# Neighbourhood attention: every second unit's probabilities turned by VectorE squares and a way through DRAM, its values product two steps later

## The chip, the cores and the metric

One Trainium2 chip, one of its cores. The kernel is a single program on that core, with every engine programmed by hand. The metric is the device time of one execution in microseconds (us), as the median of several runs. Engines are called PE (TensorE), DVE (VectorE), ACT (ScalarE), POOL (GpSimd) and SP (SyncE); SP and ACT can also issue DMAs.

## The reference, cut to what matters

The model is a block of four mixers (pool, neighbourhood attention, convolution, pool) followed by two transformer layers, all in float32 on 256 tokens of width 1024. The change is in the neighbourhood attention, which for 16 heads of width 64 computes:

```python
s_loc = s_loc + bias[None]                       # 256 local keys, with a relative position bias
s_ctx = jnp.einsum('brqhd,bchd->bhrqc', q, kc)   # 256 context keys
logits = jnp.concatenate([s_loc, s_ctx], axis=-1)
p = jax.nn.softmax(logits, axis=-1)
p_blk = jnp.einsum('bhrqij,qjk->bhrqik', p_loc, sel)
o = jnp.einsum('bhrqik,brikhd->brqhd', p_blk, vb) + jnp.einsum('bhrqc,bchd->brqhd', p_ctx, vc)
y = (o * jax.nn.silu(g)) @ w_out
```

Each head's probabilities (256 queries by 512 keys) multiply the values. A matrix product contracts over partitions, so the probabilities, computed with queries on partitions, must first be turned so that keys lie on partitions.

## The kernel before, in words

**The stretch.** `na_layer` exists three times, once for each of ACT (L888), PE (L1659) and DVE (L2370); the engines run their own programs in order and meet through semaphores. After the input projections, the attention runs as a software pipeline of 18 steps, `for i in range(NA_UNITS + 2)`. A unit is two heads (one pair `hp = u // 2`) by one half of the queries (`u % 2`), so there are 16 units, and a unit's logits are 128 partitions by 1024 columns: two heads `c`, each with 256 local and 256 context keys.

**Step i on PE.** `na_scores(i)` (L1615) computes the logits of unit i into banks 4 and 5; `gate_part(i)` (L1717) does a part of the gate's projection; `na_turned(i - 2)` (L1630) turns unit i-2's probabilities by eight 128x128 transposes (L1636) into banks 6 and 7; `na_values(i - 3)` (L1640) multiplies unit i-3's turned probabilities, now in `pt`, with the values (eight matmuls, L1655). In step 8 the gate part comes last. After steps 16 and 17 and a few gate transposes, `out_group` begins the output projection.

**Step i on DVE.** It adds the bias to the local logits of unit i and writes them to a row buffer (L2452), takes the negative maximum (L2456), copies half of unit i-2's turned probabilities from bank 6 to `pt` (`turned`, L2399), takes a reciprocal (L2403), and copies unit i-3's values product out (`values`, L2392). Steps 10 and 12 have a piece of the gate's scaling ahead of `turned` (`gate_scaled`, L2426).

**Step i on ACT.** It copies unit i's context logits to the row buffer (L904), takes the exponentials of unit i-1 (two of 512 columns, L912), copies the other half of unit i-2's turned probabilities from bank 7 to `pt` (L923), and in even steps takes one weight group apart (`split`, L654). Steps 7 and 15 have a part of the gate (L885).

**Buffers.** Row buffers are three, taken by `u % 3`; `pt` holds two units, taken by `u % 2`, so that the copies of unit u wait for the values product of unit u-2:

```python
act.wait_ge(pe_done, pe_s.count(("na_t", u, 1)))
if u >= 2:
    act.wait_ge(pe_done, pe_s.count(("na_out", u - 2)))
act.activation(pt[:, (u % 2) * 1024 + 512:(u % 2) * 1024 + 1024], ps[:, 7, :],
```

**The bias.** SP's queue loads the bias of a head pair in eight DMAs of 64 KB with rows of 256 bytes (`load_bias`, L446) into one of two halves of `bias`. The half for pair j+2 is loaded once the addition of unit 2j+1 is done (L565), POOL then adds the mask to it (L623), and DVE's addition of unit 2j+4 waits for that. Between them SP sends the output weights (`raw<-in_na_w_out`, 512 KB each) and, at two places (j = 1 and 3), a table of 1280 + 256 KB from DRAM to DRAM (`keep_rel`, L530). The last of the kernel's weights follow as slots come free.

## Time and profile before

| | us |
|---|---|
| median of 3 runs | 1818.37 (1818.0 to 1819.73) |
| span of the profiled execution | 1816.7 |
| busy: PE | 1797.5 (99%) |
| busy: POOL, DVE, ACT | 1365.0, 942.8, 905.1 |
| the 18 steps of the attention | 303.1 to 374.7 of the span |

The span runs from the first to the last instruction of the one execution that was taken with a profile; that execution's time as the runs are timed is not recorded, so the span and the median stand beside each other: 1816.7 and 1818.37. The chain of waits is the profile's answer to what ended last: it is followed back from the last instruction, at each step to what released it. TensorE's granted clock is 1.00 of full speed (2.4 GHz) in each ten-microsecond stretch from 300 to 390 us. In the views a "wait" names what ended the idle time just before an instruction.

### The profile page before, as it was taken

The numbers are of one execution on the slowest core, as the hardware profiler recorded it, in microseconds if no ns is written. First come the engines' busy times: TensorE is split into PE (matmuls) and PEld (weight loads), VectorE is DVE, ScalarE is ACT, GpSimd is POOL, SyncE is SP. The second block draws the span as 40 slices with busy tenths as digits, with TensorE's granted clock in tenths as the row PEclk, the third lists the DMA queues.
The fourth block names the chain that finished last, engine by engine and source line by source line (L and its number), as shares of the span: only waits on it lengthen the run. The fifth ranks groups of instructions, "written<-read, shape, count | busy, mean of one in ns | idle before, by whom it ended". The sixth has DMA issues, their size and how long they took to land.

```text
span 1816.7 us, 25068 instructions
## 1 busy us (share of the span) xinstructions
PE 1797.5 (99%) x9322; PEld 1482.3 (82%) x9322; DVE 942.8 (52%) x1756; ACT 905.1 (50%) x1337; POOL 1365.0 (75%) x568
## 2 busy tenths in 40 slices
PE   6999999999999999999999999999999999999999
PEld 5888888887889888887888888888888878888887
DVE  4673766678655524776553230714095865143152
ACT  3334424764456644455554644464445565545442
POOL 2624544559868898987689798969897858888885
PEclk9999999999999999999999999999999999999999
DMA  9853885748775775565466566567655645656653
GB/s 366 299 201 93 278 301 164 196 157 301 245 279 188 221 216 194 172 209 165 132 187 195 175 195 195 193 184 232 195 195 181 186 139 163 194 160 211 190 194 128
DMA packets 200697, 366.61 MB, mean 202 GB/s; under 512 B 32868, under 2 KB 54356, under 8 KB 200020
## 3 DMA queue, kind: packets, MB, share of 16 engines
q1 hardware_dynamic: 197568, 357.39, 61.6%
q10 hardware_dynamic: 3028, 7.86, 1.1%
q8 instruction: 65, 1.06, 0.2%
q14 instruction: 36, 0.29, 0.0%
HBM read 364.12 MB, written 6.13 MB: 204 GB/s over the span
## 4 chain that ended last, share of the span: by engine, by line
PE 98%; DMA 0%; ACTq 0%; ACT 0%; DVE 0%; POOL 0%; issue 0%; DVEq 0%
PE ps L1258 26%; PE ps L1260 26%; PE ps L1259 26%; PE ps L1384 3%; PE ps L1385 3%; PE ps L1386 3%; PE ps L1949 1%; PE ps L1951 1%; PE ps L1950 1%; PE ps L1306 1%; PE ps L1876 1%; PE ps L1655 1%; PE ps L1626 1%; PE ps L1636 1%; PE ps L1516 1%; PE ps L1921 1%
## 5 line engine op out<-in xcount | busy, mean ns | idle before, releaser
L616 POOL TENSOR_TENSOR w_lo<-raw,w_hi 128x1024 fp32r<-128x1024 f32 x556 | 1346.0, 2458 | 403.4 <-ACT w_hi L654 382.2
L1258 PE MATMUL ps<-w_hi,act_rows_r 128*128 128x512 f32 x2064 | 814.8, 395 | 3.2 <-POOL w_lo L616 3.1
L1260 PE MATMUL ps<-w_hi,act_rows_r 128*128 128x512 f32 x2064 | 804.8, 390 | 0.0
L1259 PE MATMUL ps<-w_lo,act_rows_r 128*128 128x512 f32 x2064 | 804.5, 390 | 0.0
L654 ACT ACTIVATE w_hi<-raw 128x1024 fp32r<-128x1024 f32 x556 | 571.1, 1058 | 359.4 <-DMA raw<-in_ffn_w_up 96.5
L1258 PEld LDWEIGHTS ps<-w_hi,act_rows_r 128*128 128x128 f32 x2064 | 387.9, 188 | 89.9 <-issue 8.6
L1260 PEld LDWEIGHTS ps<-w_hi,act_rows_r 128*128 128x128 f32 x2064 | 387.8, 188 | 81.8
L1259 PEld LDWEIGHTS ps<-w_lo,act_rows_r 128*128 128x128 f32 x2064 | 388.1, 188 | 77.2
L2604 DVE STREAM_TRANSPOSE ps<-proj 32x256 f32<-32x256 f32 (+1 forms) x384 | 166.6, 434 | 6.5
L2585 DVE TENSOR_TENSOR proj<-proj,ps 128x1024 f32<-128x1024 f32 (+1 forms) x18 | 20.4, 1132 | 252.2 <-PE ps L1260 247.8
L1384 PE MATMUL ps<-act_rows_r,w_hi 128*128 128x512 f32 (+1 forms) x288 | 101.4, 352 | 0.0
L1385 PE MATMUL ps<-act_rows_r,w_lo 128*128 128x512 f32 (+1 forms) x288 | 100.3, 348 | 0.0
L1386 PE MATMUL ps<-act_rows_r,w_hi 128*128 128x512 f32 (+1 forms) x288 | 100.2, 348 | 0.0
L1384 PEld LDWEIGHTS ps<-act_rows_r,w_hi 128*128 128x128 f32 x288 | 54.4, 189 | 8.3 <-issue 1.4
L1386 PEld LDWEIGHTS ps<-act_rows_r,w_hi 128*128 128x128 f32 x288 | 54.4, 189 | 7.0
L1385 PEld LDWEIGHTS ps<-act_rows_r,w_lo 128*128 128x128 f32 x288 | 54.4, 189 | 6.6
L2924 DVE TENSOR_TENSOR proj<-proj,ps 128x1024 f32<-128x1024 f32 x12 | 14.7, 1221 | 85.3 <-PE ps L1951 85.3
L2223 DVE SCALAR_TENSOR_TENSOR x_res<-ps,x_res 128x512 f32<-128x512 f32 x23 | 15.8, 689 | 77.3 <-PE ps L1260 77.3
L1056 ACT ACTIVATE proj<-ps 128x1024 f32<-128x1024 f32 x20 | 20.6, 1028 | 64.7 <-PE ps L1260 64.7
L985 ACT ACTIVATE proj<-ps 128x1024 f32 (+1 forms) x15 | 15.4, 1028 | 71.2 <-PE ps L1260 71.2
L2587 DVE SCALAR_TENSOR_TENSOR proj<-ps,rstat,proj 128x512 f32<-128x512 f32 (+1 forms) x12 | 7.9, 703 | 76.2 <-PE ps L1260 74.6
L2070 DVE SCALAR_TENSOR_TENSOR ps<-pt,cond,ps 128x512 f32<-128x512 f32 x60 | 45.3, 755 | 3.5 <-DMA pt<-in_ada_w 0.2
(245 smaller groups left out, 1559.9 us busy)
## 6 DMA issues: line engine op xcount, KB each, us to landing
raw<-in_w_in SPq DMA_DIRECT2D x120, 512.0 KB, 3.8
raw<-in_ffn_w_gate SPq DMA_DIRECT2D x88, 512.0 KB, 4.3
raw<-in_ffn_w_up SPq DMA_DIRECT2D x88, 512.0 KB, 4.3
raw<-in_ffn_w_down SPq DMA_DIRECT2D x88, 512.0 KB, 3.4
proj<-in_ada_w SPq DMA_DIRECT2D x39, 512.0 KB, 7.8
pt<-in_ada_w SPq DMA_DIRECT2D x38, 512.0 KB, 6.4
raw<-in_pool_w_in SPq DMA_DIRECT2D x32, 512.0 KB, 7.4
raw<-in_na_w_in SPq DMA_DIRECT2D x32, 512.0 KB, 5.4
```

The source lines that it names most:

```text
L616: pool.tensor_tensor(w_lo[:, s, :], raw[:, s, :], w_hi[:, s, :].bitcast(F32), ALU.subtract).then_inc(lo_done, 1)
L654: act.activation(w_hi[:, g % SLOTS, :], raw[:, g % SLOTS, :], ACT.Copy).then_inc(hi_done, 1)
L1056: act.activation(pj(MIX_ORDER[n] * 512, 512, IN_COLS), pair_of(n), how).then_inc(acc_free[(b + n) % 2], 1)
L1258: pe.matmul(o, h, hi, start=start, stop=False)
L1259: pe.matmul(o, h, lo, start=False, stop=False)
L1260: return pe.matmul(o, c, hi, start=False, stop=stop)
L1384: pe.matmul(o, weights_of(w_hi), high, start=start, stop=False, skip_group_check=True)
L1385: pe.matmul(o, weights_of(w_lo), high, start=False, stop=False, skip_group_check=True)
L1386: return pe.matmul(o, weights_of(w_hi), low, start=False, stop=stop, skip_group_check=True)
L2070: last = dve.scalar_tensor_tensor(out=to, in0=w, scalar=scale, in1=acc, op0=ALU.mult, op1=ALU.add)
L2585: return dve.tensor_tensor(h, h, ps[:, at:at + 2, cols_of], ALU.mult)
L2604: last = dve.transpose(to, rows)
```

## The change

`NA_SQUARED = (0, 2, 4, 6, 8, 10)` names six of the 16 units. For such a unit u:

- PE's eight transposes in step u+2 are left out, and with them both copies to `pt`.
- In their place DVE, in step u+2, turns the unit's 128x1024 probabilities by squares of 32x32 within each quadrant of partitions, one instruction, from the row buffer to `bias[:, 2048:3072]`.
- ACT, in step u+3, issues one DMA of 512 KB from there to a DRAM buffer `na_squares` (`keep_squares`), once the squares are made and the last unit's squares have come back.
- ACT, in step u+4, waits for that DMA and issues four DMAs of 128 KB with runs of 1 KB, each to 32 partitions of a buffer in `proj` (`place_squares`), which puts the squares where a full turn would.
- PE's values product of u comes in step u+5, not u+3, and waits for the four. Step 15 holds two products, of units 10 and 12; for unit 10 the output goes to bank 3.
- ACT's copy of context logits in step u+3 reuses the row buffer and waits for the squares.
- SP waits for all six DMAs to DRAM before the load of the gate rows into the same part of `bias`.

```diff
-            return 2 if u < NA_UNITS - 3 else 4
+            return 3 if u == NA_SQUARED[-1] else 2 if u < NA_UNITS - 3 else 4
+        def na_due(i):
+            return [u for u in range(NA_UNITS - 1) if u + (5 if u in NA_SQUARED else 3) == i]
...
+            sp.wait_ge(na_kept, 16 * len(NA_SQUARED))
             gate_rows(1, ((bias, 2048),), 4 * max(ADA_AT["na_in"].values()) + 3)
...
+                def keep_squares(u):
+                    act.wait_ge(dve_done, dve_s.count(("na_sq", u)))
+                    if u:
+                        act.wait_ge(na_placed, 64 * (u // 2))
+                    act.dma_start(na_squares[:], bias[:, 2048:3072]).then_inc(na_kept, 16)
+                def place_squares(u):
+                    act.wait_ge(na_kept, 16 * (u // 2 + 1))
+                    if u:
+                        act.wait_ge(pe_done, pe_s.count(("na_out", u - 2)))
+                    for kq in range(4):
+                        act.dma_start(na_placed_rows([[256, 4], [1, 256]], 0, slice(32 * kq, 32 * kq + 32)),
+                                      bass.AP(na_squares.tensor, 256 * kq, [[1024, 32], [32 * 1024, 4], [1, 256]])).then_inc(na_placed, 16)
...
-                        if i >= 3:
+                        if i - 3 in NA_SQUARED:
+                            act.wait_ge(dve_done, dve_s.count(("na_sq", i - 3)))
+                        elif i >= 3:
                             act.wait_ge(pe_done, pe_s.count(("na_t", i - 3, 1)))
...
+                    if i - 3 in NA_SQUARED:
+                        keep_squares(i - 3)
+                    if i - 4 in NA_SQUARED:
+                        place_squares(i - 4)
...
-                        act.wait_ge(pe_done, pe_s.count(("na_t", u, 1)))
-                        if u >= 2:
-                            act.wait_ge(pe_done, pe_s.count(("na_out", u - 2)))
+                        if u not in NA_SQUARED:
+                            act.wait_ge(pe_done, pe_s.count(("na_t", u, 1)))
+                            if u >= 2:
+                                act.wait_ge(pe_done, pe_s.count(("na_out", u - 2)))
...
-                pe.wait_ge(dve_done, dve_s.count(("na_pt", u, 0)))
-                pe.wait_ge(act_done, act_s.count(("na_pt", u, 1)))
+                if u in NA_SQUARED:
+                    pe.wait_ge(na_placed, 64 * (u // 2 + 1))
+                else:
+                    pe.wait_ge(dve_done, dve_s.count(("na_pt", u, 0)))
+                    pe.wait_ge(act_done, act_s.count(("na_pt", u, 1)))
...
-                    if i >= 2:
+                    due = na_due(i)
+                    for u in due[:-1]:
+                        na_values(u)
+                    if i >= 2 and i - 2 not in NA_SQUARED:
                         na_turned(i - 2)
-                    if i >= 3:
-                        na_values(i - 3)
+                    for u in due[-1:]:
+                        na_values(u)
...
+                    if u in NA_SQUARED:
+                        dve.wait_ge(act_done, act_s.count(("na_e", u, 1)))
+                        if u:
+                            dve.wait_ge(na_kept, 16 * (u // 2))
+                        dve.transpose(free(bias[:, 0:1], [[32, 8], [256, 4], [1, 32]], 2048),
+                                      na_rows_of(u, [[P, 8], [32, 4], [1, 32]])).then_inc(dve_done, dve_s.one(("na_sq", u)))
```

The order of instructions moves at two places of note. The first is DVE in step 12, before (its addition, L2452, its maximum, the gate's scaling, the copy of unit 10, reciprocal, copy of a values product):

```order
L2452 TENSOR_TENSOR full<-ps,bias 128x2x256 [waits pe_done,act_done,bias_masked]
L2456 TENSOR_REDUCE stat<-full 128x2 [waits dve_done]
L2426 SCALAR_TENSOR_TENSOR proj<-proj,rstat 128x256 [waits dve_done,acc_free0]
L2426 SCALAR_TENSOR_TENSOR proj<-proj,rstat 128x256
L2399 COPY pt<-ps 128x512 [waits pe_done]
L2403 RECIPROCAL rstat<-stat 128x2 [waits act_done]
L2392 COPY proj<-ps 128x128 [waits pe_done]
```

and with the change:

```order
L2507 TENSOR_TENSOR full<-ps,bias 128x2x256 [waits pe_done,act_done,bias_masked]
L2511 TENSOR_REDUCE stat<-full 128x2 [waits dve_done]
L2481 SCALAR_TENSOR_TENSOR proj<-proj,rstat 128x256 [waits dve_done,acc_free0]
L2481 SCALAR_TENSOR_TENSOR proj<-proj,rstat 128x256
L2448 STREAM_TRANSPOSE bias<-full 128x8x4x32 [waits na_kept,act_done]
L2458 RECIPROCAL rstat<-stat 128x2 [waits act_done]
L2439 COPY proj<-ps 128x128 [waits pe_done]
```

The copy to `pt`, which waited for PE, has become the transpose by squares, which waits for unit 10's exponentials and for the earlier DMA to DRAM.

The second is ACT from the start of step 14 to the exponentials of step 15, before (L904 copies context logits, L912 are exponentials, L923 copies unit 12 to `pt`, L654 splits weights):

```order
L904 ACTIVATE proj<-ps 128x2x256 [waits pe_done]
L912 ACTIVATE full,stat<-full,stat 128x512 [waits dve_done]
L912 ACTIVATE full,stat<-full,stat 128x512
L923 ACTIVATE pt<-ps 128x512 [waits pe_done]
L654 ACTIVATE w_hi<-raw 128x1024 [waits raw_in4]
L904 ACTIVATE full<-ps 128x2x256 [waits pe_done]
L912 ACTIVATE proj,stat<-proj,stat 128x512 [waits dve_done]
L912 ACTIVATE proj,stat<-proj,stat 128x512
```

and with the change (the same are now L939, L947, L963 and L671):

```order
L939 ACTIVATE proj<-ps 128x2x256 [waits pe_done]
L947 ACTIVATE full,stat<-full,stat 128x512 [waits dve_done]
L947 ACTIVATE full,stat<-full,stat 128x512
L929 DMA proj<-na_squares 32x4x256 [waits pe_done,na_kept]
L929 DMA proj<-na_squares 32x4x256 x3
L963 ACTIVATE pt<-ps 128x512 [waits pe_done]
L671 ACTIVATE w_hi<-raw 128x1024 [waits raw_in4]
L939 ACTIVATE full<-ps 128x2x256 [waits pe_done]
L947 ACTIVATE proj,stat<-proj,stat 128x512 [waits dve_done]
L947 ACTIVATE proj,stat<-proj,stat 128x512
```

Ahead of unit 12's copy stand now the four DMAs that bring unit 10's squares back (two rows). The copy of unit 12 still waits for PE's values product of unit 10, which has moved from step 13 to step 15.

## Rows read from the trace of the kernel before

**Rows 1.** The page, part 4: the chain that ended last, by engine.

```profile
PE 98%; DMA 0%; ACTq 0%; ACT 0%; DVE 0%; POOL 0%; issue 0%; DVEq 0%
```

**Rows 2.** PE in order of time, one step: start us, us, engine, line, what.

```profile
321.24 0.39 PE L1626 MATMUL ps<-act_rows_r 64*128 64x256 f32 x2
323.64 1.04 PE L1636 MATMUL ps<-ident,full 128*128 128x128 f32 x8
324.60 1.09 PE L1655 MATMUL ps<-pt,proj 128*64 128x128 f32 x16
325.63 0.39 PE L1626 MATMUL ps<-act_rows_r 64*128 64x256 f32 x2
```

**Rows 3.** DVE in order of time, the additions that begin steps 5, 8, 9, 12, 13.

```profile
322.98 0.69 DVE L2452 TENSOR_TENSOR proj<-ps,bias 128x512 f32<-128x512 f32 x1 [1.33 <-ACT proj L904]
323.71 1.22 DVE L2456 TENSOR_REDUCE stat<-proj 128x2 f32<-128x1024 f32 x1
337.04 0.69 DVE L2452 TENSOR_TENSOR proj<-ps,bias 128x512 f32<-128x512 f32 x1 [1.08 <-POOL bias L623]
340.70 0.69 DVE L2452 TENSOR_TENSOR full<-ps,bias 128x512 f32<-128x512 f32 x1 [0.85 <-ACT full L904]
354.70 0.69 DVE L2452 TENSOR_TENSOR full<-ps,bias 128x512 f32<-128x512 f32 x1 [2.12 <-POOL bias L623]
356.57 1.06 DVE L2426 SCALAR_TENSOR_TENSOR proj<-proj,rstat 128x256 f32<-128x256 f32 x2
358.41 0.68 DVE L2452 TENSOR_TENSOR full<-ps,bias 128x512 f32<-128x512 f32 x1
```

**Rows 4.** Busy time by stretch: us, PE, PEld, DVE, ACT, POOL, clock, DMA share, GB/s.

```profile
323.70:331.60 7.90, 7.90 (x82) 6.53 (x81) 5.05 (x9) 5.25 (x12) 3.78 (x2) 1.00 0.71 230
341.40:349.00 7.60, 7.60 (x80) 6.29 (x79) 5.62 (x11) 4.95 (x11) 2.91 (x2) 1.00 0.98 216
```

**Rows 5.** POOL in order of time: the mask that step 12 waits for.

```profile
352.28 2.40 POOL L623 TENSOR_TENSOR bias<-bias,na_mask 128x1024 f32<-128x1024 f32 x1 [7.96 <-DMA bias<-na_rows]
```

**Rows 6.** VectorE transposes by form: busy us, mean ns | idle before.

```profile
L2604 DVE STREAM_TRANSPOSE ps<-proj 32x256 f32<-32x256 f32 x320 | 145.9, 456 | 5.6
L2604 DVE STREAM_TRANSPOSE ps<-proj 32x128 f32<-32x128 f32 x64 | 20.7, 323 | 0.9
```

**Rows 7.** DMA issues: out<-in, queue, count, KB each, median us to landing.

```profile
raw<-in_na_w_out SPq DMA_DIRECT2D x8, 512.0 KB, 3.8
bias<-na_rows SPq DMA_DIRECT2D x48, 64.0 KB, 2.7
out<-x_res SPq DMA_DIRECT2D x3, 256.0 KB, 2.0
proj<-in_decay ACTq DMA_DIRECT2D x4, 192.0 KB, 4.2
```

**Rows 8.** ACT and its DMA queue (ACTq) in order of time.

```profile
52.66 3.90 ACT L654 ACTIVATE w_hi<-raw 128x1024 fp32r<-128x1024 f32 x4 [1.55 <-issue]
834.85 0.45 ACTq L659 DMA_DIRECT2D proj<-in_decay  x1
834.92 0.40 ACT L1065 ACTIVATE full<-full,stat 128x128 f32<-128x128 f32 x1
```

**Rows 9.** ACT in order of time, steps 14 to 16.

```profile
364.44 0.60 ACT L923 ACTIVATE pt<-ps 128x512 f32<-128x512 f32 x1 [0.45 <-PE ps L1636]
364.94 1.05 ACT L654 ACTIVATE w_hi<-raw 128x1024 fp32r<-128x1024 f32 x1
366.37 0.60 ACT L904 ACTIVATE full<-ps 128x512 f32<-128x512 f32 x1 [0.39 <-PE ps L1626]
370.98 0.20 ACT L912 ACTIVATION_READ_ACCUMULATOR full<-full,stat 128x1 f32 x1
```

**Rows 10.** PE in order of time: the start of step 15, and what follows the loop.

```profile
365.36 0.38 PE L1626 MATMUL ps<-act_rows_r 64*128 64x256 f32 x2
374.74 0.50 PE L1258 MATMUL ps<-w_hi,act_rows_r 128*128 128x512 f32 x1
```

More of the change, by code:

```diff
@@ L86 @@
 NA_UNITS = 16
+NA_SQUARED = (0, 2, 4, 6, 8, 10)
 NA_Z_BANK = (3, 5, 6, 7)
@@ L169, in program @@
     rel_rows = nc.dram_tensor("rel_rows", (LAYERS, P, REL_PITCH), F32, kind="Internal").ap()
+    na_squares = nc.dram_tensor("na_squares", (P, 1024), F32, kind="Internal").ap()
     gate_scratch = nc.dram_tensor("gate_scratch", (DEPTH, KC, 2, P), F32, kind="Internal").ap()
@@ L230, in program @@
         decay_in = sem("decay_in")
+        na_kept, na_placed = sem("na_kept"), sem("na_placed")
         out_done = sem("out_done")
@@ L298, in na_out_bank, with na_last_of, na_placed_rows @@
         def na_out_bank(u):
-            return 2 if u < NA_UNITS - 3 else 4
+            return 3 if u == NA_SQUARED[-1] else 2 if u < NA_UNITS - 3 else 4
+        def na_due(i):
+            return [u for u in range(NA_UNITS - 1) if u + (5 if u in NA_SQUARED else 3) == i]
+        def na_last_of(k):
+            return 4 * k + 2 if 4 * k + 2 in NA_SQUARED else 4 * k + 3
+        def na_placed_rows(dims, at=0, rows=slice(0, P)):
+            return free(proj[rows, 0:1], dims, CTX_RES + D + at)
         def na_rows_of(u, dims, at=0):
@@ L919, in na_layer @@
                         u = i - 2
-                        act.wait_ge(pe_done, pe_s.count(("na_t", u, 1)))
-                        if u >= 2:
-                            act.wait_ge(pe_done, pe_s.count(("na_out", u - 2)))
-                        act.activation(pt[:, (u % 2) * 1024 + 512:(u % 2) * 1024 + 1024], ps[:, 7, :],
-                                       ACT.Copy).then_inc(act_done, act_s.one(("na_pt", u, 1)))
+                        if u not in NA_SQUARED:
+                            act.wait_ge(pe_done, pe_s.count(("na_t", u, 1)))
+                            if u >= 2:
+                                act.wait_ge(pe_done, pe_s.count(("na_out", u - 2)))
+                            act.activation(pt[:, (u % 2) * 1024 + 512:(u % 2) * 1024 + 1024], ps[:, 7, :],
+                                           ACT.Copy).then_inc(act_done, act_s.one(("na_pt", u, 1)))
                         if i == NA_UNITS:
@@ L1654, in na_values @@
                         o = (u % 2) * 1024 + c * 512 + k * P
-                        last = pe.matmul(ps[c * HD:(c + 1) * HD, bank, 0:P], v, pt[:, o:o + P], start=k == 0, stop=k == 3)
+                        maps = na_placed_rows([[256, 4], [1, 32]], 32 * (4 * c + k)) if u in NA_SQUARED else pt[:, o:o + P]
+                        last = pe.matmul(ps[c * HD:(c + 1) * HD, bank, 0:P], v, maps, start=k == 0, stop=k == 3)
                 last.then_inc(pe_done, pe_s.one(("na_out", u)))
@@ L2395, in turned @@
                 def turned(u):
-                    dve.wait_ge(pe_done, pe_s.count(("na_t", u, 0)))
-                    if u >= 2:
-                        dve.wait_ge(pe_done, pe_s.count(("na_out", u - 2)))
-                    dve.tensor_copy(pt[:, (u % 2) * 1024:(u % 2) * 1024 + 512], ps[:, 6, :]).then_inc(dve_done, dve_s.one(("na_pt", u, 0)))
+                    if u in NA_SQUARED:
[4 more added lines that the diff above has]
+                                      na_rows_of(u, [[P, 8], [32, 4], [1, 32]])).then_inc(dve_done, dve_s.one(("na_sq", u)))
+                    else:
+                        dve.wait_ge(pe_done, pe_s.count(("na_t", u, 0)))
+                        if u >= 2:
+                            dve.wait_ge(pe_done, pe_s.count(("na_out", u - 2)))
+                        dve.tensor_copy(pt[:, (u % 2) * 1024:(u % 2) * 1024 + 512], ps[:, 6, :]).then_inc(dve_done, dve_s.one(("na_pt", u, 0)))
                     dve.wait_ge(act_done, act_s.count(("na_e", u, 1)))
@@ L2433, in gated @@
                     dve.wait_ge(pe_done, pe_s.count(("tp", "nag", 0, k)))
-                    dve.wait_ge(dve_done, dve_s.count(("na_o", 4 * k + 3)))
+                    dve.wait_ge(dve_done, dve_s.count(("na_o", na_last_of(k))))
                     z = ps[:, NA_Z_BANK[k], :].rearrange("p (c n) -> p c n", c=2)
@@ L2447, in na_layer @@
                         dve.wait_ge(pe_done, pe_s.count(("na_s", i)))
-                        if i >= 3:
+                        if i >= 3 and i - 3 not in NA_SQUARED:
                             dve.wait_ge(pe_done, pe_s.count(("na_t", i - 3, 1)))
@@ L2465, in na_layer @@
                         gate_made(7)
-                    if i >= 3:
-                        values(i - 3)
+                    for u in na_due(i):
+                        values(u)
                     if i == NA_UNITS // 2 - 1:
```

## The prediction

> **What bounds the kernel now.** I read the chain that ended last first: TensorE (PE) makes up 98% of it [rows 1], so only what shortens or stalls PE counts. The change touches one stretch, the 18 steps of the neighbourhood attention. In PE's order of time a step takes 4.39 us (321.24 to 325.63): scores and a gate part 2.40, the eight transposes 0.96, the values 1.03 [rows 2]. PE has no gap there. But two waits of VectorE (DVE) show who stands close behind. The additions that begin steps 8 and 12 stood idle 1.08 and 2.12 us for the bias that GpSimd masks [rows 3], and GpSimd in turn had waited 7.96 us for the bias loads [rows 5]. PE did not feel it: the addition of step 12 ended at 355.39, the scores of step 13 began about 1.2 us later (365.36 less two steps of 4.39). So PE bounds the stretch with the bias loads 1.2 us behind, and these loads have company: in their two slow stretches the DMA engines are busy 0.71 and 0.98 of the time [rows 4].
>
> **What is removed.** Eight transposes for each of six units: 6 x 0.96 [rows 2] = 5.8 us of PE. With them go six copies on DVE and six on ScalarE (ACT). If PE stayed the bound up to the end this would be the result; 0.2% of this kernel, 3.6 us, is about what a measurement tells from no change.
>
> **What is added, engine by engine.** *DVE*: a transpose of 128x1024 by squares. The trace has none so wide; 256 columns take 456 ns and 128 take 323 [rows 6], so 1.04 ns a column and 0.456 + 768 x 0.00104 = 1.25 us. Below it is bounded by 1.0, above by 2.4 (if it had to sit out a GpSimd operation of 2.40 us [rows 5]); the slope is the nearest, I take 1.25. It replaces a copy of about 0.6, so a pair of steps gains 0.65 us on DVE, which idles 1.33 before a plain step's addition [rows 3]: covered in plain steps. *ACT*: five DMA issues per squared unit, 0.45 us each. In the row beside it ACT computes during an issue, but four in a row left it idle for 1.55 us where nothing was queued [rows 8]. Here two exponentials stand ahead of them, and a copy of 0.6 has gone: I cost the issues at 0 (bounds 0 and 1.55 a unit; the latter would show in the slack of ACT, not at once on PE). *DMA queues*: 512 KB out and 512 KB back per squared unit, beside what SyncE's queue carries (SyncE's own new wait stands after the last bias load, ahead of a 512 KB load that nothing near needs: 0).
>
> **The way through DRAM.** Out: between 2.0 us (256 KB to DRAM in a quiet stretch) and 4.2 (192 KB, four in a row on ACT's queue); the 512 KB loads in this stretch take 3.8, which I take, as it is the same size beside the same traffic. Back: the last of four issues comes 1.35 us after the first; a landing takes between 2.7 (64 KB) and 4.2 (192 KB), 128 KB lies halfway, 3.45 [rows 7]. Together 8.6 us. There are two steps and a piece: from the end of the squares to the values some 8.1 us (for unit 10, by the steps below: 357.4 to 365.5), and one trip per pair of steps of 8.78 - 0.96 = 7.8 us, since one DRAM buffer serves all. So the trip is itself nearly the bound. The stalls at steps 8 and 12 absorb the drift of the early trips; the last counts 8.6 + 0.1 - 8.1 = 0.6 us. Bounds: 0, and with 4.2 each way over five trips (9.75 - 7.8) x 5 = 9.7.
>
> The Trainium skill (DMA: Bandwidth & Descriptors, Anatomy of one DMA) gives 2.0 us plus bytes/436 GB/s for a DMA of GpSimd's path. Estimated by that page, out takes 3.2 and back 1.35 + 2.3, together 6.9 us, and the 0.6 above would be 0.
>
> **The chain through the bias.** Call l(i) the end of the addition of step i. The loads of the bias for steps 8 and 9 start when l(5) is done, those for 12 and 13 when l(9) is.
> - l(5): before, 323.67 [rows 3]. Step 2's transposes are gone by then, and step 4's: -1.9. But ACT's copy of step 5 now waits for the squares of unit 2: l(4), a step of 4.39 ahead of l(5), comes at 319.28 - 0.96 = 318.3, the maximum (1.22, of which 1.14 count, since it overlaps its neighbours) to 319.5, squares to 320.7, copy 321.35, addition: 322.1. So -1.6.
> - l(5) to l(8) is load, mask, addition: 14.06 us (337.73 - 323.67) and does not shrink with PE. l(8) = 336.2.
> - l(8) to l(9): maximum 1.14, squares 1.25, ACT's copy 0.65, addition 0.7: 339.9 (before 341.39).
> - l(9) to l(12): again load and mask, 14.0 (355.39 - 341.39): 353.9.
> - l(12) to l(13): maximum 1.14, the gate's scaling 1.06 [rows 3], squares 1.25, copy 0.6, addition 0.7: 358.7, before 359.09.
>
> So of the 3.8 us that PE saves in steps 6 to 12 the bias gives back all but a little, and PE waits in steps 9 and 13.
>
> **The end of the loop.** Scores of step 14 start at 358.75, those of step 15 at 363.15 (before 365.36 [rows 10]): -2.2. Then a new wait. The copies of unit 12 (ACT and DVE, step 14) wait for the values of unit 10, as ever two units back; but these are now computed in step 15 and not 13. Values of unit 10: 363.15 + 2.40 + 1.03 = 366.6. Behind that wait ACT holds the copy of unit 12 (0.5), a weight split (1.05 [rows 9]) and the copy of step 15, which starts at 368.15 (before 366.37). From that copy to the end of unit 15's exponentials ACT worked without a gap for 4.8 us (366.37 to 371.18 [rows 9]): 372.95. Transposes 0.96, values 1.03: what follows the loop starts at 375.0, before at 374.74 [rows 10]: **+0.3**.
>
> **What the two share.** The new traffic meets the bias loads. At 230 GB/s and share 0.71 [rows 4] 512 KB cost all 16 engines 524/324 = 1.6 us, so the two transfers that fall into one bias load up to 3.2 us, and 0 if the engines' free time takes them. At share 0.98 there is none free: 2.0 us; at 0.71 most is: 1.0 us. Both lie on the chain above, whole: +3.0 (bounds 0 and 6.4).
>
> The Trainium skill (DMA: Bandwidth & Descriptors, Issuing engines are not separate DMA queues) says that DMAs of different issuers run on the same 16 engines and interleave, which speaks against hiding this traffic on ACT's queue. By that rule the +3.0 stands; without it the sum would be +0.9. No row here shows the two queues side by side in this stretch.
>
> **Sum**: +0.3 + 3.0 + 0.6 = +3.9 us. The profiled execution's span of 1816.7 becomes 1820.6; the runs' median, 1818.4, lies 1.7 above that span, which I take as unchanged: **1822.3 us**.
>
> **The rivals.**
> 1. *Forecast*: bias chain, tail wait, some contention. +1.5 to +6.4. Chance 0.47.
> 2. *The DMA engines have room*: shares are means, and 256-byte packets may be waiting rather than working (216 GB/s at 0.98 against 230 at 0.71). Then +0.3 to +0.9: 1819.0. For it: light stretches between loads. Against: 0.98. Chance 0.24.
> 3. *Faster*: the bias chain shrinks with PE, because its loads then overlap the other traffic less; the place is the addition of step 12. PE is free up to step 15 and only the tail wait is paid: step 15's scores at 365.36 - 5.76 = 359.6, values of unit 10 at 363.0, and by the steps above what follows at 371.4 or so: -3.3, 1815.1; it decides if the bias lands 3 us sooner after l(9). Without the tail wait too, -5.8: 1812.6. Against: 14.06 and 14.0 us in both chains. Chance 0.08.
> 4. *The trip is longer than its time*: landings of 4.2 and more each trip; PE waits before the values products of squared units, +7 to +10: 1827. For it: one DRAM buffer, and the bias loads beside it. Chance 0.16.
> 5. *Squares sit out GpSimd*: 2.4 instead of 1.25 us, three on the chain (steps 4, 8, 12), +3.5 more: 1826. Chance 0.05.
>
> **How the numbers follow.** The time is the forecast's. Faster by over 0.2% (below 1814.8): about half of rival 3, 0.04. Within 0.2%: the rest of it, rival 2 and some 0.16 of the forecast, below +3.6: 0.44. Slower (above 1822.0): the rest, 0.52. The range leaves one tenth on each side: from 1816.0 (most of rival 3 below) to 1828.5 (all but the end of rival 4).
>
> **What would show it.** PE's idle time before the scores of steps 9 and 13, released by DVE's addition and that by GpSimd's mask, 1 to 3 us each. ACT's copy of unit 12 waiting for a values product of PE, 3 us. l(5) to l(8) and l(9) to l(12) above 14 us. Squares at 1.25 us. Landings: out 3.8, back 3.5. I am wrong if PE waits instead for landed DMAs before the values in steps 5, 7, 11 (rival 4), or if these two intervals fall under 13 us (rival 3).

## The result, and the profile after

| | before | after |
|---|---|---|
| median of the runs, us | 1818.51 (4 runs, 1818.0 to 1819.73) | 1842.42 (4 runs, 1840.79 to 1847.01) |
| ratio | 1 | 1.0133 [1.0121, 1.0145] |
| span of the profiled execution, us | 1816.7 | 1845.2 (its own time 1847.01) |
| PE busy, us | 1797.5 | 1800.3 |

The change costs 23.9 us, where 3.9 were forecast and the range ended at +10. Six groups of transposes are gone, yet PE is busy 2.8 us longer, and the chain that ended last, 98% PE before [rows 1], is now 94% PE and 3% DMA (page, part 4):

```profile
PE 94%; DMA 3%; DVE 1%; ACT 1%; ACTq 1%; issue 0%; POOL 0%; DVEq 0%
```

**Where PE stood.** The waits of the stretch from 300 to 410 us (engine, what waited and for what, us in total, times, longest):

```profile
PE ps L1699 <- DMA proj<-na_squares: 19.2, 5, 8.5
ACT pt L963 <- PE ps L1699: 5.6, 1, 5.6
```

PE waited 19.2 us in five places for the rows that come back from DRAM. In PE's order of time (L1699 is a values product, L1676 and L1556 are transposes):

```profile
324.68 1.09 PE L1699 MATMUL ps<-proj 128*64 128x128 f32 x16 [1.74 <-DMA proj<-na_squares]
341.19 1.97 PE L1699 MATMUL ps<-proj 128*64 128x128 f32 x16 [8.52 <-DMA proj<-na_squares]
357.50 1.97 PE L1699 MATMUL ps<-proj 128*64 128x128 f32 x16 [6.74 <-DMA proj<-na_squares]
377.02 1.09 PE L1699 MATMUL ps<-proj 128*64 128x128 f32 x16 [1.69 <-DMA proj<-na_squares]
385.51 1.09 PE L1699 MATMUL ps<-proj 128*64 128x128 f32 x16 [0.51 <-DMA proj<-na_squares]
387.56 1.06 PE L1676 MATMUL ps<-ident,full 128*128 128x128 f32 x8 [0.95 <-DVE rstat L2458]
391.82 1.24 PE L1556 MATMUL ps<-ident,proj 128*128 128x128 f32 x8 [2.17 <-DVE proj L2439]
```

The last two waits, 3.1 us, are the tail of the loop. A values product takes 1.09 us [rows 2]; after the idle stretches of 8.52 and 6.74 us it takes 1.97. The granted clock says why (busy time by stretch: us, PE, PEld, DVE, ACT, POOL, clock, DMA share, GB/s), 1.00 before the long wait and 0.76 and 0.75 behind it, a mean of both levels, 2.4 and 1.2 GHz:

```profile
320.00:330.00 10.00, 8.26 (x86) 6.55 (x82) 6.21 (x11) 5.55 (x12) 5.15 (x3) 1.00 1.00 278
330.00:340.00 10.00, 2.67 (x18) 1.98 (x15) 3.37 (x6) 2.95 (x6) 2.47 (x3) 0.90 0.93 222
340.00:350.00 10.00, 8.80 (x71) 7.10 (x72) 5.97 (x11) 5.87 (x12) 5.90 (x3) 0.76 0.83 244
350.00:360.00 10.00, 3.26 (x29) 2.69 (x29) 2.31 (x5) 1.31 (x4) 1.56 (x2) 0.75 0.91 218
```

So a lost microsecond counts more than once: PE's busy time should have fallen by 5.8 and rose by 2.8. The Trainium skill (TensorE: Matmul & The Clock Gate, What's actually happening) names 1.2 GHz as the level of an idle array; the rows agree.

**Why the rows came late.** The chain of waits through this stretch, in order of time (start us, us, what):

```profile
324.71 9.34 DMA na_squares<-bias
334.07 0.31 ACTq L929
...
335.90 5.25 DMA proj<-na_squares
...
346.40 11.05 DMA proj<-na_squares
```

Unit 2 took 9.3 us out, 1.8 of issues, 5.3 back; unit 4's last quarter took 11.05 back. SP's queue shows what was under way at these two times (start us, us of issuing):

```profile
322.62 1.22 SPq L546 DMA_DIRECT2D rel_rows<-in_rel  x2
323.88 9.12 SPq L462 DMA_DIRECT2D bias<-na_rows  x8
345.08 1.17 SPq L546 DMA_DIRECT2D rel_rows<-in_rel  x2
```

L546 are the two copies of `keep_rel`, from DRAM to DRAM, issued within 2.1 us of the start of these two legs; behind them come bias loads. The issues of the stretch with their median landings:

```profile
na_squares<-bias ACTq DMA_DIRECT2D x6, 512.0 KB, 4.3
proj<-na_squares ACTq DMA_DIRECT2D x24, 128.0 KB, 3.7
rel_rows<-in_rel SPq DMA_DIRECT2D x2, 1280.0 KB, 9.4
```

The medians, 4.3 and 3.7, are close to the 3.8 and 3.45 that were forecast. Two of the six trips make 15.3 of the 19.2 us of waits.

**One wait far behind.** The profiled execution is the longest of the four. It holds one more wait of PE, of 2.83 us near 617 us, because one addition of DVE took 7.34 us (DVE in order of time):

```profile
609.94 7.34 DVE L3026 TENSOR_TENSOR proj<-x_res,act_rows 128x512 f32<-128x512 f32 x1
```

The same instruction takes at most 2.68 us in the trace of before, and again 7.34 us in two of the twelve experiments below (7 and 9). It belongs to the layer after, so I measure the attention by a landmark ahead of it: from the start of the first scores to the start of the last values product (unit 15). Before and after (PE in order of time):

```profile
303.13 0.38 PE L1626 MATMUL ps<-act_rows_r 64*128 64x256 f32 x2
...
380.41 1.09 PE L1655 MATMUL ps<-pt,proj 128*64 128x128 f32 x16
```

```profile
303.09 0.38 PE L1666 MATMUL ps<-act_rows_r 64*128 64x256 f32 x2
...
404.09 1.09 PE L1699 MATMUL ps<-pt,proj 128*64 128x128 f32 x16
```

That is 77.3 us and 101.0 us, +23.7, as much as the change in the medians (+23.9). PE waited 23.0 of the 101.0 us and worked 78.0; the same work took 72.6 us at a granted clock of 1.00 (experiment 8). So some 5.4 us of the loss are clock.

### The profile page after: what moved, and what is told of

It is laid out like the page before. It is cut to its first block, busy times and chain, and to the rows that moved or that the text cites. A ratio compares the mean times of both kernels' runs of the same rounds, so it can differ in the third digit from the quotient of the medians.

```text
span 1845.2 us, 24983 instructions
## 1 busy us (share of the span) xinstructions
PE 1800.3 (98%) x9274; PEld 1482.7 (80%) x9274; DVE 947.5 (51%) x1756; ACT 902.7 (49%) x1331; POOL 1364.4 (74%) x568
## 3 DMA queue, kind: packets, MB, share of 16 engines
q8 instruction: 65, 1.06, 0.2%
## 4 chain that ended last, share of the span: by engine, by line
PE 94%; DMA 3%; DVE 1%; ACT 1%; ACTq 1%; issue 0%; POOL 0%; DVEq 0%
PE ps L1298 25%; PE ps L1300 25%; PE ps L1299 25%; PE ps L1424 3%; PE ps L1425 3%; PE ps L1426 3%; PE ps L1996 1%; PE ps L1998 1%; PE ps L1346 1%; PE ps L1997 1%; DMA proj<-na_squares 1%; DMA na_squares<-bias 1%; PE ps L1923 1%; PE ps L1556 1%; PE ps L1968 1%; PE ps L1699 1%
## 5 line engine op out<-in xcount | busy, mean ns | idle before, releaser
L671 ACT ACTIVATE w_hi<-raw 128x1024 fp32r<-128x1024 f32 x556 | 571.5, 1058 | 380.1 <-DMA raw<-in_ffn_w_up 101.2
L2270 DVE SCALAR_TENSOR_TENSOR x_res<-ps,x_res 128x512 f32<-128x512 f32 x23 | 15.9, 689 | 78.6 <-PE ps L1300 78.6
L640 POOL TENSOR_TENSOR bias<-bias,na_mask 128x1024 f32<-128x1024 f32 x8 | 19.1, 2388 | 46.8 <-DMA bias<-na_rows 46.8
```

Source lines behind the costliest of these rows:

```text
L671: act.activation(w_hi[:, g % SLOTS, :], raw[:, g % SLOTS, :], ACT.Copy).then_inc(hi_done, 1)
```

## The experiments

Every number of the first column is the landmark distance less the 77.3 of before; the second is the difference of the medians, measured on the same chip. PE's idle time is from 300 to 400 us. The landmark rests on one profiled execution each: the three kernels in which PE waits for nothing there (before, 3 and 6) agree within 0.03 us, but two kernels with the trip (5 and 9), whose programs are the same up to step 13, are 2.5 us apart by then. A difference of two or three microseconds between kernels with the trip is therefore no finding by itself.

| | landmark | median | ratio [95%] | PE idle | clock 300 to 400 |
|---|---|---|---|---|---|
| the change | +23.7 | +23.9 | 1.0133 [1.0121, 1.0145] | 23.1 | 0.91 |
| 1 no trip | +7.6 | +7.4 | 1.0035 [1.0021, 1.0049] | 7.9 | 0.95 |
| 2 copies later | +14.5 | +24.4 | 1.0137 [1.0120, 1.0154] | 14.3 | 0.95 |
| 3 before, copies later | 0.0 | +8.4 | 1.0046 [1.0029, 1.0063] | 0 | 1.00 |
| 4 before, with the traffic | +5.6 | +6.6 | 1.0036 [1.0021, 1.0050] | 3.8 | 0.98 |
| 5 copies at the end | +16.3 | +16.3 | 1.0088 [1.0066, 1.0109] | 15.9 | 0.95 |
| 6 before, copies at the end | 0.0 | -0.4 | 0.9990 [0.9980, 0.9999] | 0 | 1.00 |
| 7 as 5, no trip | -1.0 | +2.1 | 1.0012 [1.0001, 1.0022] | 3.8 | 1.00 |
| 8 as 7, tail freed | -4.0 | -3.7 | 0.9984 [0.9974, 0.9994] | 0.8 | 1.00 |
| 9 as 5, tail freed | +8.2 | +12.1 | 1.0064 [1.0049, 1.0079] | 9.7 | 0.97 |
| 10 three units, u + 6 | +8.2 | +7.9 | 1.0043 [1.0029, 1.0057] | 7.0 | 0.97 |
| 11 three units, u + 5 | +4.9 | +6.3 | 1.0039 [1.0026, 1.0053] | 6.2 | 1.00 |
| 12 three units, u + 6, bank 3 | -0.1 | -0.4 | 0.9997 [0.9988, 1.0006] | 2.1 | 1.00 |

In the profiled executions of 7 and 9 the addition above took 7.34 and 7.35 us, in all others 2.7 or less; in 2 and 3 the loss behind the landmark has a cause of its own, told there.

**1. The way through DRAM taken out.** The five DMAs of a unit and their waits go; PE waits for the squares instead, and the products of the six units read what lies in the buffer, so their part of the output is not computed.

```diff
-                    act.dma_start(na_squares[:], bias[:, 2048:3072]).then_inc(na_kept, 16)
...
-                    for kq in range(4):
-                        act.dma_start(na_placed_rows(...), ...).then_inc(na_placed, 16)
...
-                    pe.wait_ge(na_placed, 64 * (u // 2 + 1))
+                    pe.wait_ge(dve_done, dve_s.count(("na_sq", u)))
```

> The change without its ten-DMA way: neither the DMA to DRAM nor the four back are issued, nobody waits for them, and the values products of the six squared units read what lies in the placed buffer (so their part of the output is not computed). Theory A (the trip through DRAM is what costs): PE's 40 us of waiting for na_squares goes, what is left is the forecast without contention, +0.3 us, so 1818 to 1821. Theory B (the rest of the change costs: squares on DVE, the bias loads behind the addition, the late values of unit 10): it stays above 1830.

1825.93 us (1822.99 to 1827.29), between the two theories. (The 40 us of the expectation add the waits of PE and of its weight loads, which overlap; PE waited 19.2.) The trip is 16.1 of the 23.7 us. But even without it the change is slower than before. The tail's two waits, 3.1 us, are still there, and another reason stands in two rows, POOL's mask for step 8 and the addition that it releases:

```profile
336.33 2.34 POOL L640 TENSOR_TENSOR bias<-bias,na_mask 128x1024 f32<-128x1024 f32 x1 [7.85 <-DMA bias<-na_rows]
338.70 0.69 DVE L2497 TENSOR_TENSOR proj<-ps,bias 128x512 f32<-128x512 f32 x1 [4.70 <-POOL bias L640]
```

PE waited 3.83 us for this addition. From l(5) to l(8) it is 17.0 us where I had kept 14.06. The addition of step 5 is done 1.3 us sooner than before, at 322.36, but SP's queue is still issuing a weight load and the two copies of `keep_rel`, and the bias load goes out at 323.83, as it did before (323.70). Its mask starts 12.5 us after that, where before it was 10.9.

**2 and 3. The copies of `keep_rel` moved** behind the convolution's first weights, in the change and in the kernel before.

```diff
-                if j in (1, 3):
-                    keep_rel(j // 2)
...
             gate_rows(2, ((pt, 0),), 4 * max(ADA_AT["cv_in"].values()) + 1)
+            keep_rel(0)
+            keep_rel(1)
```

> The change, with the two DRAM-to-DRAM table copies (1280 + 256 KB each) moved from the attention to after the convolution's weights. Theory A1 (the trips of units 2 and 6 are long because these copies and the bias loads fill the DMA engines): landings of the DMA to DRAM fall from 9.3 us at most to about 4.5, PE's waits of 8.5 and 6.7 us to about 2 each, and the time to about 1826. Theory A2 (a trip is too long for its two steps whatever runs beside it: 4.3 + 1.35 + 3.7 = 9.4 us against 7.8): the waits spread evenly, 1.5 us a unit, and the time is 1828 to 1832. Theory A3 (the copies play no part, the bias loads do): nothing changes, 1840.

> The kernel before, with the same two copies moved. PE was the bound with the bias 1.2 us behind, so all theories say no change, 1818 to 1819; what it gives is how long the bias takes from the addition to the mask without the copies: I expect 7 to 8 us in place of 10.9 for the third and fifth load.

1842.98 and 1826.98 us, neither as expected. The attention itself gains 9.2 us (23.7 to 14.5) with the copies away, but the place is a bad one: the kernel before loses 8.4 us by it while its attention is the same to 0.1 us. Its loss is for the most part a wait of PE for an operation of ACT, 6.0 us long, that ends at 519 us, in the layer after (5.7 in experiment 2). So these two medians say nothing of the change; the landmark does, and 5 and 6 repeat the pair with another place.

What 3 was made for came as expected. With the copies away, POOL's mask for step 8 starts 8.0 us after the bias load goes out (323.81), where before it was 10.9 (334.63 less 323.70), and that for step 12 after 7.0 instead of 10.9:

```profile
331.80 2.39 POOL L623 TENSOR_TENSOR bias<-bias,na_mask 128x1024 f32<-128x1024 f32 x1 [3.69 <-DMA bias<-na_rows]
```

**4. The traffic alone, beside the kernel before.** DMAs of the same sizes at the same steps, from and to buffers that nobody on PE or DVE waits for. The way back reads an input, and the way out has six buffers in DRAM, so it waits for nothing.

```diff
+                    if i - 3 in (0, 2, 4, 6, 8, 10):
+                        act.dma_start(na_squares[i // 2 - 1], bias[:, 2048:3072]).then_inc(na_kept, 16)
+                    if i - 4 in (0, 2, 4, 6, 8, 10):
+                        if i > 4:
+                            act.wait_ge(na_placed, 64 * (i // 2 - 2))
...
```

> The kernel before (all 16 units turned by PE) with the change's DMA traffic beside it and nobody on PE or DVE waiting for it: six DMAs of 512 KB from SBUF to DRAM on ACT's queue in steps 3 to 13 and six times four of 128 KB from DRAM in steps 4 to 14 (from an input, into a buffer nobody reads; each four wait for the four before). Forecast's contention term: the bias comes 1 to 2 us later in two places with 1.2 us to spare, so +1 to +3 us. Theory A1: the landings in steps 5 and 9 are 8 to 10 us here as well. If they are 4 us here, it is not the company that made them long in the change.

1825.13 us, +6.6 where +1 to +3 was expected. This is the disputed term by itself. The bias came later, and PE, bound by nothing before, now waited 3.23 us for an addition (POOL, DVE and PE in order of time):

```profile
339.23 2.34 POOL L626 TENSOR_TENSOR bias<-bias,na_mask 128x1024 f32<-128x1024 f32 x1 [10.02 <-DMA bias<-na_rows]
341.60 0.69 DVE L2463 TENSOR_TENSOR proj<-ps,bias 128x512 f32<-128x512 f32 x1 [5.46 <-POOL bias L626]
342.44 0.39 PE L1637 MATMUL ps<-act_rows_r 64*128 64x256 f32 x2 [3.23 <-DVE proj L2463]
```

Landings in this run (DMA issues, KB each, median us):

```profile
raw<-in_na_w_out SPq DMA_DIRECT2D x8, 512.0 KB, 6.9
bias<-na_rows SPq DMA_DIRECT2D x48, 64.0 KB, 5.2
na_squares<-bias ACTq DMA_DIRECT2D x6, 512.0 KB, 7.5
```

Against 3.8 and 2.7 of before [rows 7] both of SP's kinds of load take 2.5 to 3.1 us longer. The chains l(5) to l(8) and l(9) to l(12) are 18.5 and 16.5 us, 4.4 and 2.5 longer than before. The queues do share their engines, as the Trainium skill has it (DMA: Bandwidth & Descriptors, Issuing engines are not separate DMA queues); here the ways out don't wait for the trip before, as they do in the change, so that this kernel may well show more pressure on the bias than the change has. The way out took 10.2 us in step 5 and 8.6 in step 9, beside the copies, 6.5 to 7.7 in steps 7, 11 and 13, and 3.3 in step 3: the long leg does not need the change's own waits.

**5 and 6. The copies at the end of the attention's loads**, ahead of the convolution's weights, in the change and in the kernel before.

```diff
             keep_gates(2)
+            keep_rel(0)
+            keep_rel(1)
             narrow(I["conv_w_in"]
```

> The change, with the two DRAM-to-DRAM table copies moved to the end of the attention's sends, where the DMA engines are 0.2 to 0.3 busy (in the earlier place, after the convolution's weights, they cost 6 us of their own there). The earlier run's attention stretch had PE waits on landed squares of 3.7 us at most in place of 8.5, so: time 1842 - 24 + about 13 = 1830 to 1833. If the copies' company is not what makes the trips long, 1840 or more.

> The kernel before with the same move: PE is bound there, 1818 to 1819 if the new place costs nothing; a loss here has to be taken off the other three runs of this set.

1835.19 and 1818.56 us. The place is free this time, so the pair stands: without the company of the copies the loss is 7.5 us less. No landing of the trip is above 6.2 us now, and yet PE waits for five trips of six, four of them early ones (PE in order of time):

```profile
324.11 1.09 PE L1699 MATMUL ps<-proj 128*64 128x128 f32 x16 [1.29 <-DMA proj<-na_squares]
335.61 1.09 PE L1699 MATMUL ps<-proj 128*64 128x128 f32 x16 [3.51 <-DMA proj<-na_squares]
346.45 1.09 PE L1699 MATMUL ps<-proj 128*64 128x128 f32 x16 [1.32 <-DMA proj<-na_squares]
357.85 1.98 PE L1699 MATMUL ps<-proj 128*64 128x128 f32 x16 [3.41 <-DMA proj<-na_squares]
```

Pairs of steps follow at 11.5, 10.8 and 11.4 us here, by these rows, where 7.8 was to be had. That is the true length of a trip with one buffer. The next way out is issued 0.03 us after the values product starts (335.64, 346.48, 357.88), since both wait for the same four DMAs; so the round is the way out, the issues and the landing of the last quarter: 3.0, 1.8 and 6.0 us for the round that ends at 346.45. The last of the four landed after 4.9, 6.0 and 6.2 us in these three rounds, while the median of all 24 is 3.9.

The clock fell behind both long waits. Behind the one at 357.85 the values product is slow at once; behind the one at 335.61 it is the next product, and the two pairs of steps, less their waits, took 9.5 us each, against 8.0 behind the two waits of 1.3 us (PE, then busy time by stretch):

```profile
337.77 1.97 PE L1699 MATMUL ps<-pt,proj 128*64 128x128 f32 x16
```

```profile
338.00:340.00 2.00, 2.00 (x17) 1.67 (x16) 1.66 (x3) 1.88 (x5) 0.00 (x0) 0.50 0.69 140
358.00:360.00 2.00, 2.00 (x18) 1.67 (x20) 0.13 (x1) 0.60 (x1) 0.00 (x0) 0.50 0.86 276
```

One wait in this trace has another cause. In step 12 DVE's two scalings of the gate took 3.84 us, where the change has 0.75 and the kernel before 1.06 [rows 3], and PE waited for the copy behind them (DVE, then PE). Experiment 2 has the same, 3.86 and 2.04 us.

```profile
363.96 3.84 DVE L2481 SCALAR_TENSOR_TENSOR proj<-proj,rstat 128x256 f32<-128x256 f32 x2
369.34 1.09 PE L1699 MATMUL ps<-proj 128*64 128x128 f32 x16 [2.02 <-DVE proj L2439]
```

Without it the copies' company would come out some 2 us larger than 7.5.

**7 and 8. No trip, the copies at the end, and then the tail freed.** In 8 the copies to `pt` of unit u no longer wait for the values of unit u-2 where that is squared, since it has not used `pt`.

```diff
-                            if u >= 2:
+                            if u >= 2 and u - 2 not in NA_SQUARED:
                                 act.wait_ge(pe_done, pe_s.count(("na_out", u - 2)))
```

> No DMA out and back (the values of squared units read what lies in the placed buffer, so their part is not computed), and the copies at the end. With the copies beside it this was 1825.9, with 17.0 and 18.3 us between the additions of steps 5 and 8, and 7 and 10. Theory: the bias loads, not DVE's squares, were what PE waited for; without the copies the bias takes 8 us and no step waits for it, and only the late values of unit 10 are left of the loss: -5.8 + 3 to 4, so 1815 to 1817. If the squares on DVE or ACT's order cost by themselves: 1820 or more.

> As the run before, and the copies to pt no longer wait for the values of a squared unit two back (which doesn't use pt): this frees unit 12's copies in step 14 from the values of unit 10 in step 15. Theory (the tail's wait was worth 3 to 4 us of PE time): 1812 to 1813.5, the full 5.8 us of the transposes. If that wait was hidden: the same as the run before.

Both leave out the trip, and with it the six units' part of the output. 1821.02 us (1817.96 to 1825.19) and 1815.20 us (1814.44 to 1820.03), 4.0 and 1.7 us above the ends of what was expected. By the landmark the tail's wait is 3.0 us (-1.0 against -4.0), and the rows of 7 show it as PE's idle time in step 16 and behind it, with ACT's copy of unit 12 before (ACT, then PE):

```profile
363.43 0.60 ACT L955 ACTIVATE pt<-ps 128x512 f32<-128x512 f32 x1 [5.07 <-PE ps L1691]
364.27 1.06 PE L1668 MATMUL ps<-ident,full 128*128 128x128 f32 x8 [0.95 <-DVE rstat L2448]
368.54 1.07 PE L1548 MATMUL ps<-ident,proj 128*128 128x128 f32 x8 [2.17 <-DVE proj L2431]
```

The medians differ by 5.8. The profiled execution of 7 has the long addition of DVE on top, and its fastest execution is only 3.5 us above the fastest of 8; whether the addition makes the rest of the 5.8 in the executions without a profile isn't shown. Experiment 8 is what the removed transposes are worth when nothing takes their place: 4.0 us, not 5.8. From the first scores to those of step 15 six transposes and the one product put off should be 6.8 us less; it is 5.2. A later step without transposes takes 3.52 us, 0.87 less than 4.39 and not 0.96 (0.45 over five steps), and 1.2 are lost in steps 2 and 3, where PE runs into DVE's addition:

```profile
316.07 0.39 PE L1658 MATMUL ps<-act_rows_r 64*128 64x256 f32 x2 [0.48 <-DVE full L2497]
```

**9. As 5, with the tail freed.** The edit of 8 in kernel 5, the trip kept.

> The changed kernel with the two keep_rel copies moved behind keep_gates(2), as in the run that gave 1835.2, and besides the copies to pt no longer wait for a squared unit's values (they were in no need of it: a squared unit doesn't use pt). Theory A (the trip is late in each pair of steps and sets PE's time up to its last one; the wait of unit 12's copies is paid after that, on top of it): the 5.8 us that the same edit took away without the trip come off here too: 1829 to 1830. Theory B (the tail's wait lies beside the late trips; it costs only what the trips leave): 1832 to 1835, and PE's waits for the landed rows grow by what the tail's wait loses.

1830.75 us (1830.03 to 1832.13), 4.4 below the median of 5, with the long addition in its profile. The landmark fell by 8.1 us, from +16.3 to +8.2. Not all of that is the edit's. It touches the copies of unit 12 alone, in step 14, and from the first scores to the values product of step 13 it is 66.4 us in 5 and 63.8 in 9. These 2.5 us are scatter, most of it PE's wait for DVE in step 13 of 5. Behind that product it is 27.2 and 21.6 us. These 5.5 us can be the edit's: the tail's two waits (3.1), two waits of 0.2 and 0.4 ahead of them, and 1.9 of clock, which fell to 0.50 at 386 to 388 us in 5 and stayed at 1.00 in 9. In 7 the same two waits cost no clock (1.00 from 368 to 380). The last trips' waits of 9:

```profile
356.89 1.09 PE L1699 MATMUL ps<-proj 128*64 128x128 f32 x16 [2.44 <-DMA proj<-na_squares]
366.97 1.09 PE L1699 MATMUL ps<-proj 128*64 128x128 f32 x16 [0.57 <-DMA proj<-na_squares]
```

Against 8, which differs from 9 by the trip alone, the trip costs 12.2 us where neither the copies nor the tail add to it: 9.0 of waits and 3.2 of clock.

**10 and 11. Three units instead of six**, 0, 4 and 8, with the values at u + 6 and at u + 5, both with the copies at the end and the tail freed.

```diff
-NA_SQUARED = (0, 2, 4, 6, 8, 10)
+NA_SQUARED = (0, 4, 8)
-            return 3 if u == NA_SQUARED[-1] else 2 if u < NA_UNITS - 3 else 4
+            return 2 if u < NA_UNITS - 3 else 4
-            return [u for u in range(NA_UNITS - 1) if u + (5 if u in NA_SQUARED else 3) == i]
+            return [u for u in range(NA_UNITS - 1) if u + (6 if u in NA_SQUARED else 3) == i]
```

> As the run before, but only units 0, 4 and 8 go through squares and DRAM, and their values follow three steps later than before the change (at step u + 6), so that a trip has some 12.5 us in place of 8.1, and the buffers one trip per four steps (some 17 us). Removed: 3 x 0.96 = 2.9 us of PE. Theory A (what is lost is the trip's time against its steps and nothing else): no wait of PE for landed rows at all, 1818.6 - 2.9 = 1815.7, within 0.5. Theory B (every trip also costs by ACT's held issues and by its packets beside the bias loads, which delay the masks): 1817 to 1820, with masks more than 1 us later than without. Theory C (12.5 us are still too few in company): PE waits for landed rows, 1820 or more.

> The same three units 0, 4 and 8, but with their values at step u + 5, as in the change: only the trip's time is as short as there, the buffers have room. Theory A (one DRAM buffer per pair of steps is what makes the trips late, each waiting for the one before): no wait of PE, 1815.7 as with u + 6. Theory B (a single trip alone is longer than its 8.1 us in this company, whatever the buffers): PE waits 0.5 to 3.5 us in each of steps 5, 9 and 13, 1818 to 1822.

1826.55 and 1824.88 us, slower than expected. With 12.5 us for a trip PE never waits for DRAM, but it loses as much elsewhere, by a wait of my own making: at u + 6 two values products fall into one step with no transposes between them, and both go to bank 2, so the second waits for DVE to copy the first out, behind its addition, maximum and squares. It did so in two steps, 6 and 10, 3.23 and 2.29 us (in step 14, where transposes lie between, PE waits 0.70 us for ACT; the expectation of experiment 12 counts one wait of 3.2 us too many). The first (PE of experiment 10 in order of time):

```profile
332.77 1.60 PE L1700 MATMUL ps<-pt,proj 128*64 128x128 f32 x16 [3.23 <-DVE proj L2440]
```

At u + 5, with a free DRAM buffer each time, the first trip is still 2.06 us late and the third 0.62 (PE of experiment 11):

```profile
324.87 1.09 PE L1700 MATMUL ps<-proj 128*64 128x128 f32 x16 [2.06 <-DMA proj<-na_squares]
361.83 1.09 PE L1700 MATMUL ps<-proj 128*64 128x128 f32 x16 [0.62 <-DMA proj<-na_squares]
```

So the trip is longer than two steps by itself, and the single buffer only adds to it. Of the 6.2 us of idle time in 11 these two waits are 2.7; four waits for ACT's copies to `pt` are another 2.6.

**12. As 10, with the squared units' values in bank 3.**

```diff
-            return 2 if u < NA_UNITS - 3 else 4
+            return 3 if u in NA_SQUARED else 2 if u < NA_UNITS - 3 else 4
```

> The same three units 0, 4 and 8 with their values at step u + 6, as in the run that gave 1826.6, but a squared unit's values go to bank 3. In that run PE never waited for landed rows; it waited 3.2, 3.2 and 2.3 us for DVE's copy of the first of two values products that fall into one step (steps 6, 10, 14), as both used bank 2 and no transposes lie between. Theory A (that is its whole loss): the three waits go, 1815.7 to 1817, faster than before by 0.1 to 0.15%, and the masks no longer late. Theory B (the trips' packets delay the masks even when nobody waits for the trip): PE waits for DVE's additions at steps 8 and 12, 1818 to 1820.

1818.26 us (11 runs), ratio 0.9997 [0.9988, 1.0006]: no difference that can be measured. No wait for DRAM and none for bank 2 is left. Of the 2.9 us of transposes PE gives back 2.1 in small waits for DVE and ACT and 0.7 more that no wait shows. The largest wait:

```profile
334.61 1.06 PE L1677 MATMUL ps<-ident,full 128*128 128x128 f32 x8 [0.88 <-ACT pt L964]
```

No version of the change that computes the whole output beats the kernel before; only 8, which leaves the trip out, is faster (0.9984).

## Why the prediction was wrong

The landmarks take the change apart into four terms, each the difference of two kernels: the removal -4.0 (experiment 8 against before), the tail's wait +3.0 (7 against 8), the company of the copies +8.6 (1 against 7), the trip +16.1 (the change against 1). They add up to 23.7 by construction, and the order matters: beside the trip the tail is worth 5.5 (5 against 9, behind step 13), the copies 7.5 (the change against 5), and the trip without the other two 12.2 (9 against 8). The bias chain, on which the forecast rested, released no wait of PE in the change. The prediction's own sign of being wrong, PE waiting for landed DMAs, came in steps 5, 7, 9, 13 and 15.

- **The way through DRAM: the step that failed.** "Together 8.6 us" against "some 8.1" gave +0.6; the bound with landings of 4.2 each way gave 9.7. Shown: 16.1, and 12.2 without the copies and the tail. Three things were missing. First, I took the landings from medians of a stretch and put every trip at the median; the medians were right (4.3 and 3.7 for 3.8 and 3.45), but two legs, beside a `keep_rel` copy and a bias load, took 9.3 and 11.05. The whole lateness of one trip is paid, and an early one earns nothing. Second, the way back is four DMAs, and PE waits for the last to land: in run 5, without the copies, that one took 4.9 to 6.2 us and not 3.45, so that three rounds in a row took 10.8 to 11.5 us and not 8.6. The sum had counted the last trip alone, with 0.6 us. Third, PE's clock fell behind the long waits (5.4 us in the change), a term that the sum did not have. Rival 4 had the mechanism and the buffer, and a chance of 0.16, but its price of +7 to +10 was built on landings no longer than 4.2, the longest row that I had looked for; the landings of the copies themselves, 8.7 and 10.3 us in the trace of before, would have been a better end.
- **The page's rule.** The Trainium skill's 2.0 us plus bytes/436 GB/s (DMA: Bandwidth & Descriptors, Anatomy of one DMA) makes the leg out 3.2 us, an estimate from a figure for GpSimd's path. In the change the shortest way out on ACT's queue was 3.0, the longest 9.3: it fits a quiet moment and says nothing of a busy one.
- **What the two share: under-sized.** Forecast 1.0 + 2.0; shown by experiment 4 as 4.4 + 2.5 in the two chains, 5.6 us by the landmark, with trips that wait for less than the change's do. I took the first chain, with a DMA share of 0.71, for the roomier one; it was the worse.
- **The chain through the bias: a bound only without the trip, and not a fixed length.** In the change PE waited for the trip and never for the bias. "14.06 us and does not shrink with PE" holds only with the copies in it. In 1 it grew to 17.0; with the copies moved (7) it is 11.3 to 11.9 and PE no longer waits for it. By experiment 3 the copies make 3 of the 10.9 us from the load to the mask in the kernel before, and 4 in the second chain.
- **The end of the loop: right.** Forecast: ACT's copy of unit 12 waits for the values of unit 10, and costs 2.5 us against a loop without that wait. Shown: waits of 5.07 (7) and 5.64 us (the change), 3.0 us by the landmark without the trip and 5.5 beside it.
- **Squares: right.** 1.23 to 1.25 us each, forecast 1.25; rival 5 did not occur for them. Another DVE instruction was held up in runs 2 and 5 (3.84 us for 1.06 or less), which no rival had.
- **ACT's issues: costed at 0, wrong in places.** The row ahead of a weight split at 321.05 has 2.04 us of idle time behind four issues, above my bound of 1.55, and the chain that ended last runs through these four (ACT and its queue in order of time):

```profile
319.11 1.89 ACTq L929 DMA_DIRECT2D proj<-na_squares  x4
321.05 1.06 ACT L671 ACTIVATE w_hi<-raw 128x1024 fp32r<-128x1024 f32 x1 [2.04 <-issue]
```

- **What is removed: 5.8 forecast, 4.0 shown** (experiment 8: steps 2 and 3, and 0.87 a step for 0.96).

## What to carry to other kernels

A transfer with a date is priced at its longest landing in the worst company that it meets, not at the median, because a late one is paid in full and an early one earns nothing; where several DMAs must all have landed, the last of them counts. Where one buffer serves a series of trips, write out the whole round (out, issue, back, start of the next) and compare that with the period, before comparing one trip with its slack. The long landings of a trace of before, of whatever transfer, are the rows to look for. And a lookahead edit has two more clients to check: waits written as "two units back", whose meaning moves with the product, and PSUM banks, where two products now fall into one step.

## What the runs showed of the hardware

- A DMA of 512 KB from SBUF to DRAM landed in 3.0 to 9.3 us, and one of 128 KB back in 2.5 to 11.1, in one kernel, by what was in flight beside it.
- Waits of PE of 3.51 and 3.41 us (before 335.61 and 357.85 in run 5) cost 1.5 us of clock each beyond their own length: the pairs of steps behind them took 9.5 us without waits, against 8.0 behind waits of 1.29 and 1.32. The clock can fall after the first product behind the wait, so that product alone doesn't tell: it was at full speed at 335.61, and the next took 1.97. In run 9 waits of 3.42 and 2.44 us cost the same 1.5 and one of 2.21 none.
- One DVE addition of 128x512 with all operands in SBUF took 0.68, 2.7 or 7.34 us. In the trace of the change it lies inside a stretch in which POOL worked without a gap (twelve weight splits in 28.34 us from 588.39); but so does the one of 2.68 us in the trace of before (eight in 19.81 us from 573.95), so such a stretch alone doesn't make the 7.34. What holds DVE up was not tested. It happened in three of fourteen profiled executions. The span of these three exceeds that of before by 4.7 to 5.4 us more than the landmark does, in the others (2 and 3 aside) by 1.0 at most; single executions of the kernel before near 1823 us may be the same, which stays open.
- Four DMAs of 128 KB issued one after another do not land alike: the median of 24 was 3.9 us in run 5, the last of a four up to 6.2.
